# A layer norm's variance summed with tokens on the partitions, and its reciprocal spread by diagonals and a product with ones

## The chip, the cores and the metric

The kernel runs on one core of one Trainium2 chip. The metric is the device time of one execution in microseconds (us). The engines are TensorE (PE in the profile, PEld its weight loads), VectorE (DVE), ScalarE (ACT), GpSimd (POOL) and SyncE (SP, which here only issues DMAs).

## The reference

A two-layer trunk over 512 frames and 16 meta tokens, 528 tokens of 1024 channels in fp32. Layer 0 mixes with a convolution group and a pooling group, layer 1 with gated linear attention, and a squared-ReLU MLP follows each. The change lies in layer 0's mixer. Cut to what matters:

```python
a = a_in[..., :CONV_DIM] * jax.nn.sigmoid(a_in[..., CONV_DIM:])
a = causal_depthwise_conv(a, conv_w, conv_b)          # 512 channels, 31 taps
a = jax.nn.silu(layer_norm(a, ln_g, ln_b))            # mean and variance over the 512 channels of each token
...
return jnp.concatenate([a, p], axis=-1) @ w_out       # p: the pooling group's 512 channels
# layer_norm: xc * rsqrt(mean(xc * xc) + EPS) * g + b
```

## The kernel before

**Layout.** Activations lie with channels on the 128 partitions and the 528 tokens along the free dimension, so `conv` is four tiles of 128x528 (CT = 4) and a sum over channels is a sum over the four tiles and over the partitions. Each exact fp32 product is three passes over a split of both operands: weights `w_hi`, `w_lo` and activations `a_hi`, `a_lo` (`exact`, L1872), where ScalarE makes the hi part of a half block of weights (`split_hi`, L525) and VectorE the lo part (`split_lo`, L532).

**PSUM.** It is cut into NS = 4 slots of two banks. `plan_slots` numbers every accumulator of the program in the order in which TensorE fills them, and the n-th lies in slot n % 4. `start_slot(n)` makes TensorE wait until accumulator n-4 has been read: the semaphore `evac0` to `evac3` of that slot, which the engine that reads an accumulator last increments. `filled(eng, n)` is the wait in the other direction. So which read a TensorE tile waits for is set by its distance of four in that order alone.

**Order.** Each engine's program is written out by hand and runs in order. Around the change TensorE fills, in this order: `outp` 0 to 2 (the output projection of the pooling half, one 128x528 tile of 24 matmul instructions for each k), `mean`, `outp` 3 and 4, `var`, `outp` 5 to 7, then `outc` 0 to 7 (the same projection of the convolution half, which needs the normed convolution as `a_hi`, `a_lo`), then the MLP of layer 0. With the accumulator of `mean` called m, these are `outp` 3 = m+1, `outp` 4 = m+2, `var` = m+3, `outp` 5 = m+4, `outp` 6 = m+5, `outp` 7 = m+6, `outc` 0 = m+7, `outc` 1 = m+8.

**The norm.** VectorE subtracts the mean from the four tiles (L1421), ScalarE squares them (L880), VectorE adds the squares to one tile `centred_sq_sum` (L1425, L1429, a part of `h_sq`). TensorE multiplies it with `ones_c`, a 128x128 tile of 1/512 (`plain`, L1880), which leaves the variance of each token in all 128 partitions. ScalarE takes the root of that 128x528 tile into `std` (L886), VectorE the reciprocal into `rstd` (`recip`, L1252) and multiplies the four tiles with it (L1436). ScalarE applies Silu (L889), and for each of the four tiles VectorE makes `a_lo` (L1442) and, but for the first, `a_hi` (L1440). TensorE starts `outc` 0 with a wait for the first `a_lo` (`c_lo_ready`), and its four steps j wait for one `a_lo` each.

**The residual.** Each `outp` accumulator is added to `h` by VectorE (`add_to_h`, L1266), which frees its slot. `out_pool(k)` is this addition and, for odd k, one `split_lo`.

Of the kernel before, what the change touches and what calls it, by code (L numbers as in the profile page):

```python
# [17 lines left out]
ALU = mybir.AluOpType  # L18
ACT = mybir.ActivationFunctionType
# [91 lines left out]
def plan_slots():  # L111
# [5 lines left out]
    order += [("conv", 2)] + [("p", g) for g in range(PG)]  # L117
    order += [("mix", 0), ("mix", 1), ("conv", 3), ("mix", 2), ("mix", 3)]
    order += [("outp", k) for k in range(OUT_MEAN)] + [("mean",)]
    order += [("outp", k) for k in range(OUT_MEAN, OUT_VAR)] + [("var",)]  # L120
    order += [("outp", k) for k in range(OUT_VAR, KD)] + [("outc", k) for k in range(KD)]
    slot = {}

    def add(names):
# [83 lines left out]
def build_trunk(nc, x, meta_tokens, mix_norm_g, ffn_norm_g, ffn_w1, ffn_w2, cp_w_in, cp_conv_w,  # L208
                cp_conv_b, cp_ln_g, cp_ln_b, cp_pool_w, cp_pool_scale, cp_w_out, gla_w_in,
                gla_gate_w2, gla_gate_b, gla_head_g, gla_w_out, final_norm_g, out):  # L210
    with ExitStack() as ctx:
# [3 lines left out]
        def sem(name):  # L215
            return ctx.enter_context(nc.semaphore(name))
# [197 lines left out]
        o_sq_ready = sem("o_sq_ready")  # L414
        o_sq_summed = sem("o_sq_summed")
        diag_set = sem("diag_set")
        head_rows_ready = sem("head_rows_ready")
        head_normed = sem("head_normed")
        gated = sem("gated")
# [4 lines left out]
        dve_out = sem("dve_out")  # L424
        stored = sem("stored")
        N_CONST = 13
        WARM = 16

        def filled(eng, n):

            eng.wait_ge(filled_n, n + 1)

        def evacuated(eng, n):

            eng.wait_ge(evac[n % NS], n // NS + 1)
# [17 lines left out]
        def slot_ap(n, tokens=FULL, rows=P):  # L453
            a, b = pcols(tokens)
            return ps[0:rows, n % NS, a:b]
# [71 lines left out]
        def split_lo(n):  # L527

            dve = nc.vector
            half_free(dve, n)  # L530
            dve.wait_ge(w_hi_ready, group(n) + 1)
            dve.tensor_tensor(w_view(w_lo, n), half_view(raw, n), w_view(w_hi, n).bitcast(F32),  # L532
                              ALU.subtract).then_inc(w_lo_ready, 1)
# [203 lines left out]
        def _(act):  # L737
# [145 lines left out]
                    split_hi(2 * B_OUTC + k // 2)  # L883
            n = SLOT["var",]
            filled(act, n)
            act.activation(std[:, :], slot_ap(n), ACT.Sqrt, bias=eps[:, :]).then_inc(evac[n % NS], 1)  # L886
            for c in range(CT):
                act.wait_ge(normed, c + 1)
                act.activation(work[c], conv[:, c, :], ACT.Silu, bias=vec[:, V_LB + c:V_LB + c + 1],  # L889
                               scale=vec[:, V_LG + c:V_LG + c + 1]).then_inc(silu_ready, 1)  # L890
                if c == 0:

                    act.wait_ge(silu_ready, 1)
                    act.activation(a_hi[:, c, :], work[c], ACT.Copy).then_inc(c_hi_ready, 1)
# [314 lines left out]
        def _(dve):  # L1209
# [39 lines left out]
            def recip(n, tokens):  # L1249

                evacuated(dve, n)
                V.reciprocal(rstd[:, tokens[0]:tokens[1]], std[:, tokens[0]:tokens[1]])\  # L1252
                 .then_inc(rstd_ready, 1)
                uses[0] += 1
                dve.wait_ge(rstd_ready, uses[0])
# [154 lines left out]
            def out_pool(k):  # L1410
                add_to_h(k, SLOT["outp", k], FULL)
                if k % 2:
                    split_lo(2 * B_OUTC + k // 2)
# [12 lines left out]
            for c in range(2, CT):  # L1426
                dve.wait_ge(ln_sq_ready, c + 1)
                dve.wait_ge(ln_sq_summed, c - 1)
                V.tensor_tensor(centred_sq_sum, centred_sq_sum, work[c], ALU.add).then_inc(ln_sq_summed, 1)  # L1429
            split_lo(2 * B_OUTP + 3)  # L1430
            split_lo(2 * B_OUTC)
            for k in range(OUT_MEAN, OUT_VAR):
                out_pool(k)
            recip(SLOT["var",], FULL)
            for c in range(CT):
                V.tensor_tensor(conv[:, c, :], conv[:, c, :], rstd[:, :], ALU.mult).then_inc(normed, 1)  # L1436
            for c in range(CT):
                if c:
                    dve.wait_ge(silu_ready, c + 1)
                    V.tensor_copy(a_hi[:, c, :], work[c]).then_inc(c_hi_ready, 1)  # L1440
                dve.wait_ge(c_hi_ready, c + 1)
                V.tensor_tensor(a_lo[:, c, :], work[c], a_hi[:, c, :].bitcast(F32), ALU.subtract)\  # L1442
                 .then_inc(c_lo_ready, 1)
            for k in range(OUT_VAR, KD):
                out_pool(k)
            for k in range(KD):
# [398 lines left out]
        def _(pe):  # L1845
# [30 lines left out]
            def plain(n, pairs, tokens):  # L1876

                for i, (l, r) in enumerate(pairs):
                    for c, a, b in parts(tokens):
                        last = mm(ps[:, n % NS, c:c + b - a], l, r[:, a:b], start=(i == 0),  # L1880
                                  stop=(i == len(pairs) - 1))
                last.then_inc(filled_n, 1)
# [166 lines left out]
            for k in range(KD):  # L2049
                if k == OUT_MEAN:  # L2050

                    n = SLOT["mean",]
                    start_slot(n)
                    pe.wait_ge(conv_summed, 2)
                    plain(n, [(ones_c[:, :], late_sum), (ones_c[:, :], conv_sum)], FULL)
                if k == OUT_VAR:
                    n = SLOT["var",]
                    start_slot(n)
                    pe.wait_ge(ln_sq_summed, CT - 1)
                    plain(n, [(ones_c[:, :], centred_sq_sum)], FULL)  # L2060
                project_out0("outp", B_OUTP, k, PG, lambda j: evacuated(pe, SLOT["mix", j]))
            for k in range(KD):
                project_out0("outc", B_OUTC, k, 0, lambda j: pe.wait_ge(c_lo_ready, j + 1))
# [345 lines left out]
```

## Time and profile before

| | us |
|---|---|
| median of 3 runs | 1080.72 (1080.23 to 1080.99) |
| the profiled execution, its time | 1080.46 |
| its span, first to last instruction | 1078.7 |
| TensorE busy | 1067.3 (99%) |
| VectorE busy | 806.2 (75%) |
| ScalarE busy | 530.6 (49%) |

The span is that of the trace; the time holds 1.76 us more around it. The busy shares are averages over all stages; the change lies between 114 and 139 us of the span, and is read there. In a timeline row the first number is the start from the span's start, the second the duration of the group, and a bracket at the end is the idle time of that engine just before it. Records of one engine overlap by some hundredths, so the distance of two starts is what an instruction costs in a row of others.

### The profile page before, as it was taken

How to read it: one execution, taken by the hardware profiler on the slowest of the kernel's cores; microseconds unless marked ns; L12 is line 12 of the kernel's file. 1: busy time of each engine (PE TensorE's matmuls, PEld its weight loads, DVE VectorE, ACT ScalarE, POOL GpSimd, SP SyncE). 2: the span in 40 equal slices, each digit the busy share in tenths (PEclk: the TensorE clock that was granted, in tenths of full speed). 3: DMA queues.
4: the chain of work that ended last, by engine and by line, in shares of the span. 5: the costliest groups of instructions: out<-in, count | busy, mean ns of one | idle time of the engine just before them, and what ended most of it. 6: DMA issues, size and time to landing. Idle time of an engine off the chain costs nothing.

```text
span 1078.7 us, 19613 instructions
## 1 busy us (share of the span) xinstructions
PE 1067.3 (99%) x8190; PEld 992.5 (92%) x8190; DVE 806.2 (75%) x1161; ACT 530.6 (49%) x794; POOL 30.9 (3%) x85
## 2 busy tenths in 40 slices
PE   8999999999999999999999999999999999999997
PEld 8998999999999999999999877787898898898897
DVE  6899987876786786789563468757886896796785
ACT  7324454544454454467652256535544454454564
POOL 5050000000000000000000000000000000000000
PEclk9999999999999999999999999999999999999999
DMA  7361222234134125222232222222234135134121
GB/s 219 118 159 45 79 79 79 79 108 127 39 118 137 60 80 156 79 77 81 79 118 80 78 79 79 80 78 90 66 103 133 40 118 156 40 117 131 66 79 79
DMA packets 100469, 102.76 MB, mean 95 GB/s; under 512 B 3803, under 2 KB 96717, under 8 KB 100381
## 3 DMA queue, kind: packets, MB, share of 16 engines
q1 hardware_dynamic: 98780, 99.12, 29.5%
q0 software_dynamic: 1536, 2.32, 1.0%
q8 instruction: 65, 1.06, 0.4%
q14 instruction: 24, 0.19, 0.1%
q10 hardware_dynamic: 64, 0.07, 0.0%
HBM read 97.12 MB, written 2.10 MB: 92 GB/s over the span
## 4 chain that ended last, share of the span: by engine, by line
PE 95%; DVE 3%; ACT 1%; issue 0%; DMA 0%; DVEq 0%; ACTq 0%
PE ps L1872 56%; PE ps L2090 28%; PE ps L2161 4%; PE ps L2019 1%; PE ps L2122 1%; PE ps L1919 1%; PE ps L2254 1%; PE ps L2273 1%; PE ps L1880 1%; DVE w_lo L532 0%; ACT conv L775 0%; DMA xin<-in_x_dram 0%; PE ps L2149 0%; PE ps L2192 0%; DVE w_lo L571 0%
## 5 line engine op out<-in xcount | busy, mean ns | idle before, releaser
L1872 PE MATMUL ps<-u_lo,w_hi 128*128 128x264 f32 (+1 forms) x1120 | 299.5, 323 | 1.7 <-DVE u_lo L1299 1.7
L1872 PE MATMUL ps<-u_hi,w_hi 128*128 128x264 f32 (+1 forms) x1120 | 295.2, 320 | 0.0
L1872 PE MATMUL ps<-u_hi,w_lo 128*128 128x264 f32 (+1 forms) x1120 | 294.8, 319 | 0.0
L2090 PE MATMUL ps<-c_lo,w_hi 128*128 128x264 f32 (+1 forms) x868 | 245.9, 283 | 0.3 <-DVE w_lo L571 0.3
L2090 PE MATMUL ps<-c_hi,w_hi 128*128 128x264 f32 (+1 forms) x868 | 244.9, 282 | 0.0
L2090 PE MATMUL ps<-c_hi,w_lo 128*128 128x264 f32 (+1 forms) x868 | 244.7, 282 | 0.0
L525 ACT ACTIVATE w_hi<-raw 128x1024 fp32r<-128x1024 f32 x118 | 123.7, 1057 | 162.6 <-PE ps L1872 135.0
L1872 PEld LDWEIGHTS ps<-u_lo,w_hi 128*128 128x128 f32 x1120 | 184.8, 188 | 20.2 <-issue 4.8
L1872 PEld LDWEIGHTS ps<-u_hi,w_hi 128*128 128x128 f32 x1120 | 185.9, 188 | 16.5 <-issue 1.2
L1872 PEld LDWEIGHTS ps<-u_hi,w_lo 128*128 128x128 f32 x1120 | 185.5, 188 | 15.4
L532 DVE TENSOR_TENSOR w_lo<-raw,w_hi 128x1024 fp32r<-128x1024 f32 x118 | 143.7, 1223 | 64.8 <-ACT w_hi L525 63.1
L2090 PEld LDWEIGHTS ps<-c_lo,w_hi 128*128 128x128 f32 x868 | 163.4, 188 | 0.9 <-DVE w_lo L571 0.5
L2090 PEld LDWEIGHTS ps<-c_hi,w_hi 128*128 128x128 f32 x868 | 163.5, 188 | 0.2
L2090 PEld LDWEIGHTS ps<-c_hi,w_lo 128*128 128x128 f32 x868 | 163.3, 188 | 0.0
L932 ACT ACTIVATE c_hi<-parts 128x528 fp32r<-128x528 f32 (+3 forms) x132 | 73.4, 577 | 88.9 <-DVE parts L1500 51.4
L1487 DVE TENSOR_TENSOR c_lo<-parts,c_hi 128x528 fp32r<-128x528 f32 (+3 forms) x132 | 81.7, 625 | 30.2 <-ACT c_hi L932 23.7
L571 DVE TENSOR_TENSOR w_lo<-s_sum,w_hi 128x1024 fp32r<-128x1024 f32 x62 | 75.8, 1222 | 10.4 <-ACT w_hi L563 10.0
L1468 DVE SCALAR_TENSOR_TENSOR relu<-ps,rstd 128x528 f32<-128x528 f32 (+1 forms) x64 | 44.7, 698 | 47.3 <-PE ps L1872 47.2
L563 ACT ACTIVATE w_hi<-s_sum 128x1024 fp32r<-128x1024 f32 x62 | 65.7, 1059 | 13.5 <-PE ps L1872 9.9
L563 ACT ACTIVATE w_hi<-raw 128x1024 fp32r<-128x1024 f32 (+1 forms) x62 | 52.5, 846 | 37.7 <-PE ps L2090 30.4
L571 DVE TENSOR_TENSOR w_lo<-raw,w_hi 128x1024 fp32r<-128x1024 f32 (+1 forms) x62 | 59.1, 953 | 9.3 <-ACT w_hi L563 9.3
L1340 DVE SCALAR_TENSOR_TENSOR conv<-conv_in,cw,conv 128x528 f32<-128x528 f32 x66 | 47.0, 764 | 0.3
(266 smaller groups left out, 1306.5 us busy)
## 6 DMA issues: line engine op xcount, KB each, us to landing
raw<-in_ffn_w_dram SPq DMA_DIRECT2D x64, 1024.0 KB, 5.5
raw<-in_gla_w_in_dram SPq DMA_DIRECT2D x12, 1024.0 KB, 5.4
raw<-in_cp_w_in_dram SPq DMA_DIRECT2D x8, 512.0 KB, 5.4
raw<-in_cp_w_out_dram SPq DMA_DIRECT2D x4, 1024.0 KB, 5.2
raw<-in_gla_w_out_dram SPq DMA_DIRECT2D x4, 1024.0 KB, 5.1
shifted<-conv_in POOLq DMA_DIRECT2D x32, 69.5 KB, 2.1
xin<-in_x_dram SPq DMA_DIRECT2D x4, 512.0 KB, 5.5
raw<-in_cp_w_in_dram SPq DMA_DIRECT2D x2, 1024.0 KB, 5.0
```

The source lines that it names most:

```text
L525: act.activation(w_view(w_hi, n), half_view(raw, n), ACT.Copy).then_inc(w_hi_ready, 1)
L532: dve.tensor_tensor(w_view(w_lo, n), half_view(raw, n), w_view(w_hi, n).bitcast(F32), ALU.subtract).then_inc(w_lo_ready, 1)
L563: act.activation(hi, src, ACT.Copy).then_inc(w_hi_ready, 1)
L571: dve.tensor_tensor(lo, src, hi.bitcast(F32), ALU.subtract).then_inc(w_lo_ready, 1)
L932: act.activation(c_hi[:, first:last + 1, j, 0:w], now[:, first:last + 1, :], ACT.Copy)\
L1340: V.scalar_tensor_tensor(out=conv[:, c, :], in0=src, scalar=wt, in1=conv[:, c, :], op0=ALU.mult, op1=ALU.add).then_inc(tap_done[c], 1)
L1468: V.scalar_tensor_tensor(out=relu[:, i % 2, a:b], in0=slot_ap(n, tokens), scalar=0.0, in1=rstd[:, a:b], op0=ALU.max, op1=ALU.mult)\
L1487: V.tensor_tensor(c_lo[:, first:last + 1, j, 0:w], now[:, first:last + 1, :], c_hi[:, first:last + 1, j, 0:w].bitcast(F32), ALU.subtract)\
L1872: last = mm(ps[:, n % NS, c:c + b - a], l, r[:, a - origin:b - origin], start=(k == 0 and i == 0), stop=(k == count - 1 and i == 2))
L1880: last = mm(ps[:, n % NS, c:c + b - a], l, r[:, a:b], start=(i == 0), stop=(i == len(pairs) - 1))
L2090: last = mm(bank, l[:, 0, j, :], r, start=(fresh and j == 0 and m == 0), stop=(j == KD // 2 - 1 and m == 2), skip_group_check=not fresh)
L2161: last = mm(ps[:, n % NS, 0:256], l, r, start=(k == 0 and i == 0), stop=(k == KD - 1 and i == 2))
```

## The change

TensorE now multiplies with the operands in the other order: five matmuls, each with 128 tokens of `centred_sq_sum` as weights and one column of `ones_c` as the moving operand, give the variance with tokens on the partitions, 128x5 (`VAR_AT` holds the first token of each; the fifth overlaps the fourth and is there for the last 16 tokens). ScalarE's root and VectorE's reciprocal work on 128x5. VectorE then writes diagonals of the reciprocals into `std` (four 128x128 blocks in one instruction, and 16 columns in a second), and TensorE multiplies them with `ones_1` in a new accumulator `spread`, which holds the reciprocal of each token in all partitions. VectorE's four products read it from PSUM.

On VectorE the small reciprocal and the diagonals stand ahead of the additions of `outp` 3 and 4, `split_lo(2 * B_OUTC)` behind these, and `split_lo(2 * B_OUTC + 1)` behind the four `a_lo`. On TensorE `spread` stands between `outp` 5 and `outp` 6.

```diff
--- before.py
+++ after.py
@@ -117,8 +117,8 @@
     order += [("conv", 2)] + [("p", g) for g in range(PG)]
     order += [("mix", 0), ("mix", 1), ("conv", 3), ("mix", 2), ("mix", 3)]
     order += [("outp", k) for k in range(OUT_MEAN)] + [("mean",)]
-    order += [("outp", k) for k in range(OUT_MEAN, OUT_VAR)] + [("var",)]
-    order += [("outp", k) for k in range(OUT_VAR, KD)] + [("outc", k) for k in range(KD)]
+    order += [("outp", k) for k in range(OUT_MEAN, OUT_VAR)] + [("var",), ("outp", OUT_VAR), ("spread",)]
+    order += [("outp", k) for k in range(OUT_VAR + 1, KD)] + [("outc", k) for k in range(KD)]
     slot = {}
 
     def add(names):
@@ -414,6 +414,7 @@
         o_sq_ready = sem("o_sq_ready")
         o_sq_summed = sem("o_sq_summed")
         diag_set = sem("diag_set")
+        var_rows_ready = sem("var_rows_ready")
         head_rows_ready = sem("head_rows_ready")
         head_normed = sem("head_normed")
         gated = sem("gated")
@@ -424,6 +425,7 @@
         dve_out = sem("dve_out")
         stored = sem("stored")
         N_CONST = 13
+        VAR_AT = [P * t for t in range(TT)] + [TOK - P]
         WARM = 16
 
         def filled(eng, n):
@@ -883,9 +885,12 @@
                     split_hi(2 * B_OUTC + k // 2)
             n = SLOT["var",]
             filled(act, n)
-            act.activation(std[:, :], slot_ap(n), ACT.Sqrt, bias=eps[:, :]).then_inc(evac[n % NS], 1)
+            act.activation(std_tok[:, :], ps[:, n % NS, 0:TT + 1], ACT.Sqrt, bias=eps[:, :]).then_inc(evac[n % NS], 1)
             for c in range(CT):
-                act.wait_ge(normed, c + 1)
+                if c < CT - 1:
+                    act.wait_ge(normed, c + 1)
+                else:
+                    evacuated(act, SLOT["spread",])
                 act.activation(work[c], conv[:, c, :], ACT.Silu, bias=vec[:, V_LB + c:V_LB + c + 1],
                                scale=vec[:, V_LG + c:V_LG + c + 1]).then_inc(silu_ready, 1)
                 if c == 0:
@@ -1428,12 +1433,22 @@
                 dve.wait_ge(ln_sq_summed, c - 1)
                 V.tensor_tensor(centred_sq_sum, centred_sq_sum, work[c], ALU.add).then_inc(ln_sq_summed, 1)
             split_lo(2 * B_OUTP + 3)
+            evacuated(dve, SLOT["var",])
+            V.reciprocal(rstd_tok[:, :], std_tok[:, :]).then_inc(var_rows_ready, 1)
+            dve.wait_ge(var_rows_ready, 1)
+            V.tensor_tensor(std[:, 0:SEQ].rearrange("p (t n) -> p t n", n=P),
+                            ident[:, None, :].to_broadcast([P, TT, P]),
+                            rstd_tok[:, 0:TT, None].to_broadcast([P, TT, P]), ALU.mult).then_inc(var_rows_ready, 1)
+            V.tensor_scalar(std[:, SEQ:], ident[:, P - META:], rstd_tok[:, TT:TT + 1], None,
+                            ALU.mult).then_inc(var_rows_ready, 1)
+            for k in range(OUT_MEAN, OUT_VAR):
+                add_to_h(k, SLOT["outp", k], FULL)
             split_lo(2 * B_OUTC)
-            for k in range(OUT_MEAN, OUT_VAR):
-                out_pool(k)
-            recip(SLOT["var",], FULL)
+            n = SLOT["spread",]
+            filled(dve, n)
             for c in range(CT):
-                V.tensor_tensor(conv[:, c, :], conv[:, c, :], rstd[:, :], ALU.mult).then_inc(normed, 1)
+                V.tensor_tensor(conv[:, c, :], conv[:, c, :], slot_ap(n), ALU.mult)\
+                 .then_inc(normed if c < CT - 1 else evac[n % NS], 1)
             for c in range(CT):
                 if c:
                     dve.wait_ge(silu_ready, c + 1)
@@ -1441,6 +1456,7 @@
                 dve.wait_ge(c_hi_ready, c + 1)
                 V.tensor_tensor(a_lo[:, c, :], work[c], a_hi[:, c, :].bitcast(F32), ALU.subtract)\
                  .then_inc(c_lo_ready, 1)
+            split_lo(2 * B_OUTC + 1)
             for k in range(OUT_VAR, KD):
                 out_pool(k)
             for k in range(KD):
@@ -2057,7 +2073,15 @@
                     n = SLOT["var",]
                     start_slot(n)
                     pe.wait_ge(ln_sq_summed, CT - 1)
-                    plain(n, [(ones_c[:, :], centred_sq_sum)], FULL)
+                    for t, a in enumerate(VAR_AT):
+                        last = mm(ps[:, n % NS, t:t + 1], centred_sq_sum[:, a:a + P], ones_c[:, 0:1],
+                                  start=True, stop=True)
+                    last.then_inc(filled_n, 1)
+                if k == OUT_VAR + 1:
+                    n = SLOT["spread",]
+                    start_slot(n)
+                    pe.wait_ge(var_rows_ready, 3)
+                    plain(n, [(ones_1[:, :], std)], FULL)
                 project_out0("outp", B_OUTP, k, PG, lambda j: evacuated(pe, SLOT["mix", j]))
             for k in range(KD):
                 project_out0("outc", B_OUTC, k, 0, lambda j: pe.wait_ge(c_lo_ready, j + 1))
```

The new accumulator moves the numbers behind it: `outp` 5 = m+4 as before, `spread` = m+5, `outp` 6 = m+6, `outp` 7 = m+7, `outc` 0 = m+8, `outc` 1 = m+9.

TensorE at the start of `outc` 0, before (the waits of an instruction in brackets; `ps` is the accumulator):

```order
L1872 MATMUL ps<-a_hi,w_lo 128x264 x2
L1872 MATMUL ps<-a_lo,w_hi 128x264 [waits c_lo_ready,evac3,w_lo_ready]
L1872 MATMUL ps<-a_lo,w_hi 128x264
L1872 MATMUL ps<-a_hi,w_hi 128x264 x2
L1872 MATMUL ps<-a_hi,w_lo 128x264 x2
L1872 MATMUL ps<-a_lo,w_hi 128x264 [waits c_lo_ready]
```

and of the changed kernel at the same place:

```order
L1888 MATMUL ps<-a_hi,w_lo 128x264 x2
L1888 MATMUL ps<-a_lo,w_hi 128x264 [waits c_lo_ready,evac0,w_lo_ready]
L1888 MATMUL ps<-a_lo,w_hi 128x264
L1888 MATMUL ps<-a_hi,w_hi 128x264 x2
L1888 MATMUL ps<-a_hi,w_lo 128x264 x2
L1888 MATMUL ps<-a_lo,w_hi 128x264 [waits c_lo_ready]
```

The instruction that opens `outc` 0 waited for slot 3, which `var` had held; it now waits for slot 0, which `outp` 5 holds.

VectorE from the last `split_lo` ahead of the norm's second half to the addition of `outp` 5 and beyond, before (L1266 is the addition to `h`, L532 a `split_lo`):

```order
L532 TENSOR_TENSOR w_lo<-raw,w_hi 128x4x256 [waits w_hi_ready,filled] x2
L1266 TENSOR_TENSOR h<-h,ps 128x528 [waits filled]
L532 TENSOR_TENSOR w_lo<-raw,w_hi 128x4x256 [waits w_hi_ready,filled]
L1266 TENSOR_TENSOR h<-h,ps 128x528 [waits filled]
L1252 RECIPROCAL rstd<-std 128x528 [waits evac3]
L1436 TENSOR_TENSOR conv<-conv,rstd 128x528 [waits rstd_ready]
...
L1440 CAST a_hi<-act 128x528 [waits silu_ready]
L1442 TENSOR_TENSOR a_lo<-act,a_hi 128x528 [waits c_hi_ready]
L1266 TENSOR_TENSOR h<-h,ps 128x528 [waits filled]
L532 TENSOR_TENSOR w_lo<-raw,w_hi 128x4x256 [waits w_hi_ready,filled]
```

and now:

```order
L534 TENSOR_TENSOR w_lo<-raw,w_hi 128x4x256 [waits w_hi_ready,filled]
L1437 RECIPROCAL rstd_tok<-std_tok 128x5 [waits evac3]
L1439 TENSOR_TENSOR std<-ident,rstd_tok 128x512 [waits var_rows_ready]
L1442 TENSOR_SCALAR std<-ident,rstd_tok 128x16
L1271 TENSOR_TENSOR h<-h,ps 128x528 [waits filled] x2
L534 TENSOR_TENSOR w_lo<-raw,w_hi 128x4x256 [waits w_hi_ready,filled]
L1450 TENSOR_TENSOR conv<-conv,ps 128x528 [waits filled]
...
L1457 TENSOR_TENSOR a_lo<-act,a_hi 128x528 [waits c_hi_ready]
L534 TENSOR_TENSOR w_lo<-raw,w_hi 128x4x256 [waits w_hi_ready,filled]
L1271 TENSOR_TENSOR h<-h,ps 128x528 [waits filled]
L534 TENSOR_TENSOR w_lo<-raw,w_hi 128x4x256 [waits w_hi_ready,filled]
```

Behind the last `a_lo` there stood the addition of `outp` 5 and then a `split_lo`; now a `split_lo`, the addition of `outp` 5, and a `split_lo`.

## Rows read from the trace of the kernel before

**Rows 1.** The page: the span.

```profile
span 1078.7 us, 19613 instructions
```

**Rows 2.** The chain in order of time: start us, us, what.

```profile
116.05 2.55 DVE conv L1421 x4
...
126.09 3.37 DVE rstd L1252
...
136.00 28.01 PE ps L1872 x228
```

**Rows 3.** Timeline of TensorE, 121 to 137 us: start us, us, instruction.

```profile
121.69 1.05 PE L1880 MATMUL ps<-h_sq,ones_c 128*128 128x264 f32 x4
122.38 0.60 PE L1872 MATMUL ps<-a_lo,w_hi 128*128 128x264 f32 x2
...
125.49 0.40 PE L1872 MATMUL ps<-a_lo,w_hi 128*128 128x264 f32 x2
...
131.09 0.40 PE L1872 MATMUL ps<-a_hi,w_lo 128*128 128x264 f32 x2
132.82 0.48 PE L1872 MATMUL ps<-a_lo,w_hi 128*128 128x264 f32 x2 [1.33 <-DVE a_lo L1442]
133.14 0.40 PE L1872 MATMUL ps<-a_hi,w_hi 128*128 128x264 f32 x2
...
136.84 0.41 PE L1872 MATMUL ps<-a_lo,w_hi 128*128 128x264 f32 x2
```

**Rows 4.** Timeline of VectorE, 121 to 137 us.

```profile
121.37 2.35 DVE L532 TENSOR_TENSOR w_lo<-raw,w_hi 128x1024 fp32r<-128x1024 f32 x2
...
126.01 3.45 DVE L1252 RECIPROCAL rstd<-std 128x528 f32<-128x528 f32 x1
129.49 2.57 DVE L1436 TENSOR_TENSOR conv<-conv,rstd 128x528 f32<-128x528 f32 x4
131.97 0.70 DVE L1442 TENSOR_TENSOR a_lo<-relu,a_hi 128x528 fp32r<-128x528 f32 x1
...
135.24 0.71 DVE L1442 TENSOR_TENSOR a_lo<-act,a_hi 128x528 fp32r<-128x528 f32 x1
135.86 0.70 DVE L1266 TENSOR_TENSOR h<-h,ps 128x528 f32<-128x528 f32 x1
136.48 1.22 DVE L532 TENSOR_TENSOR w_lo<-raw,w_hi 128x1024 fp32r<-128x1024 f32 x1
```

**Rows 5.** Timeline of ScalarE: the root of the variance.

```profile
122.78 0.70 ACT L886 ACTIVATE std<-ps,eps 128x528 f32<-128x528 f32 x1 [1.25 <-PE ps L1880]
```

**Rows 6.** Timeline of TensorE in layer 1, a sum with tokens on partitions.

```profile
515.57 0.95 PE L1914 MATMUL ps<-ones_d,sq_sum 128*128 128x1 f32 x8
516.38 1.14 PE L1880 MATMUL ps<-sq_sum,ones_d 128*128 128x264 f32 x4
```

**Rows 7.** Timeline of ScalarE in layer 1, the root of that sum.

```profile
516.55 0.26 ACT L763 ACTIVATE std_tok<-ps,eps 128x4 f32<-128x4 f32 x1 [0.53 <-PE ps L1914]
```

**Rows 8.** Groups of VectorE in layer 1: busy us, mean ns of one.

```profile
L1709 DVE TENSOR_TENSOR act<-ident,rstd_head 128x512 f32<-128x512 f32 x2 | 1.4, 692 | 0.1
...
L1706 DVE RECIPROCAL rstd_head<-std_head 128x4 f32<-128x4 f32 x2 | 0.3, 174 | 0.0
```

**Rows 9.** Stretches: PE, PEld, DVE, ACT, POOL busy us, granted clock, DMA share, GB/s.

```profile
13.00:14.00 1.00, 0.00 (x0) 0.00 (x0) 1.00 (x3) 1.00 (x2) 1.00 (x3) 1.00 1.29 227
...
1073.00:1074.00 1.00, 0.00 (x0) 0.00 (x0) 0.94 (x3) 0.78 (x2) 0.00 (x0) 1.00 1.01 406
1074.00:1075.00 1.00, 0.00 (x0) 0.00 (x0) 0.43 (x2) 0.30 (x2) 0.00 (x0) 0.70 0.39 148
```

**Rows 10.** Timeline of SyncE's DMA issues, 118 to 150 us.

```profile
125.50 14.95 SPq L616 DMA_DIRECT2D raw<-in_ffn_w_dram  x2
```

**Rows 11.** Timeline of ScalarE: the first split of the MLP's weights.

```profile
145.87 1.06 ACT L525 ACTIVATE w_hi<-raw 128x1024 fp32r<-128x1024 f32 x1 [2.72 <-PE ps L1872]
```

**Rows 12.** DMA issues of the page: KB each, us to landing.

```profile
raw<-in_ffn_w_dram SPq DMA_DIRECT2D x64, 1024.0 KB, 5.5
```

## The prediction

> **What bounds the kernel now.** I began with the page's span [rows 1] and then read the chain of work in order of time, because the change touches one short stage and shares over the whole span say nothing of it. From 116.05 us the chain lies on VectorE, through the reciprocal at 126.09, up to the last `a_lo`, and from 136.00 on TensorE [rows 2]. So in this stage VectorE decides when TensorE gets its operands for `outc` 0. The price of that on TensorE is in its timeline [rows 3]: `outp` 6 and 7 take 2.92 us each (125.49 to the end of their 24 matmuls; the last pair starts at 131.09, and pairs follow each other at 0.24, so the tiles end at 131.33). `outc` 0 could start there. It starts at 132.82, after an idle time of 1.33, and then meets three more `a_lo` one by one; `outc` 1 starts at 136.84. A tile that waits for nothing takes 2.92, so 136.84 - 131.33 - 2.92 = 2.59 us are lost. That is all that a shorter VectorE chain could win here. From 136.00 TensorE is the chain for 28.01 us and 228 matmuls, 0.123 each, its own pace: a shift of `outc` 1 is carried on, neither given back nor made larger.
>
> **TensorE, what is removed and added.** `var` starts at 121.69 and `outp` 5 at 122.38, which gives 0.69 for the old product [rows 3]. The new one has the form of a sum in layer 1: four such matmuls start at 515.57 and the next work at 516.38, 0.81 for four, 0.20 each [rows 6]. Five take 1.01, so `outp` 5 starts at 122.70. Behind a plain product it took 125.49 - 122.38 = 3.11 [rows 3]; behind the small ones it is between 2.92 and 3.11, and I take 3.11: 125.81. There `spread` stands, the old form again, 0.69: `outp` 6 starts at 126.50, takes 3.11, `outp` 7 takes 2.92, and both are done at 132.53. TensorE has 1.20 us more to do ahead of `outc` 0 than before (1.0 with the lower values). Before, this would have lain inside the 2.59 lost.
>
> **The new chain to the four products.** The root can start 516.55 - 515.57 = 0.98 after four small matmuls began [rows 6, 7], with a fifth 1.18, at 122.87, and takes 0.26: 123.13. VectorE begins its last `split_lo` of this place at 121.37 and is free at 122.50 (two take 2.35, one lasts 1.22, so they follow at 1.13) [rows 4]. The reciprocal of a few columns takes 0.17, the diagonals have a twin in layer 1 with 0.69 [rows 8]; the 16 columns have none, and I bound them by the small reciprocal, 0 to 0.17. With hand-overs of 0.1 the diagonals stand at about 124.2. TensorE comes to `spread` at 125.81, so this wait isn't felt. Then VectorE adds `outp` 3 and 4 (0.62 each: 135.86 to 136.48 for one [rows 4]) and does a `split_lo`, 1.13: free at about 126.6. `spread` is readable 122.78 - 121.69 = 1.09 after it starts [rows 3, 5], at 126.90. So TensorE sets the start of the four products, at 126.90 against 129.49 before [rows 4], with VectorE 0.3 behind as the next bound. The removed reciprocal of 3.45 thus brings 2.59 us on VectorE. If the small steps cost up to 0.3 more, nothing changes; above that each tenth costs a tenth.
>
> **The products from PSUM.** Before they read both operands from SBUF, 2.57 for four [rows 4]; the subtraction of the mean has the new form, one operand from PSUM, and takes 2.55 [rows 2]. I take no difference.
> The Trainium skill (VectorE: DVE Perf Modes, the section on the TRN2 errata) gives a PSUM source a fixed cost 62 cycles of 0.96 GHz above an SBUF source. By that, an estimate of 0.26 us for the four would be added to the loss below; the rows of this trace show no such difference, and I go by them.
>
> **What TensorE then waits for.** The four `a_lo` move with the products: the first ends at 131.97 + 0.70 - 2.59 = 130.08, the last at 133.36. TensorE comes at 132.53 and needs the last one 3/4 of a tile later, at 134.7. So none of these is waited for any more. But the order fences show that the opening instruction of `outc` 0 now waits for slot 0, which `outp` 5 holds: the extra accumulator `spread` has put `outc` 0 at a distance of four from `outp` 5, where before it was `var`, long read. The read that frees it is VectorE's addition of `outp` 5. Before, this addition stood right behind the last `a_lo`, and only `outc` 1 waited for it (135.86 + 0.70 = 136.56, just ahead of 136.84). Now a `split_lo` has been moved ahead of it, and everything of the norm's chain stands there too. VectorE: after the last `a_lo` 135.86 - 2.59 = 133.27, `split_lo` 1.13, 134.40, addition 0.70, 135.10. With 0.05 to 0.15 for the hand-over (the first `a_lo` ended at 132.67 and TensorE started at 132.82 [rows 3, 4]) `outc` 0 starts at 135.20. TensorE is idle from 132.53 for 2.7 us, in one piece. Then the tile runs without a wait, 2.92 and 0.08 for the first pair after a wait (132.82 to 133.14 is 0.32 against 0.24): `outc` 1 starts at 138.20, where before it was 136.84.
>
> **The sum:** +1.36 us. The profiled execution took 1080.46, of which 1078.7 are span and the rest unchanged around it, so the changed kernel would take 1081.8; on the median of the runs, which is 0.26 above the profiled one, 1082.1. I give 1082.0. Both ends of the terms: `outp` 5 at 2.92 instead of 3.11 and a hand-over of 0.05 make +1.1; diagonals that are 0.5 late, or 0.1 more for each small step, make +1.7. For the case itself that is 1081.6 to 1082.6.
>
> **What hides the rest.** The MLP's first weights are loaded when VectorE has split both halves of the block that lay in that buffer: issued at 125.50 before [rows 10], now behind the moved `split_lo`, at about 134.4. A load lands 5.5 later [rows 12], at 140; ScalarE uses it at 145.87 when TensorE has finished `outc` 3 [rows 11], now at about 147. With this 7 us of cover gone it would cost one for one. `outp` 6 waits for the read of `outp` 4 (about 125.5, TensorE comes at 126.5), and `outc` 1 for that of `spread`, at about 129.5. ScalarE has less to do.
>
> **The rivals.** (1) *The stall doesn't bind and the shorter chain is gained.* `outc` 0 starts at 132.53 and `outc` 1 at 135.45, 1.39 earlier than before: 1079.3. For it speaks that VectorE's chain really becomes 2.59 shorter; against it, that the addition of `outp` 5 would have to be read by 132.53, 2.6 us before VectorE's program reaches it. This is the faster side; it decides only if the addition ends ahead of 132.5. (2) *The clock falls in the long wait.* In the rows the granted clock is 1.00 through the idle microsecond from 13 to 14 and through the first idle one behind the last matmul, 1073 to 1074, and 0.70 on average in the next, where it goes to the lower of its two levels [rows 9]. A wait of 2.7 us is longer than what these rows show without a fall. Its price: at 1.2 GHz pairs would start at twice 0.24, so a single tile of 2.92 costs 2.9 more: 1085.0.
> The Trainium skill (TensorE: Matmul & The Clock Gate, "Why this matters for your kernels") asks to avoid long idle gaps between bursts, since the clock gate then goes back to half rate; ahead of the fall at the end this trace has small matmuls and waits as well as the idle time, which here dense tiles replace, so I hold the fall unlikely. (3) *The loss is given back.* If TensorE had idle time behind `outc` 1 that waits for something not moved, it would be absorbed: 1080.7, no change. The 228 matmuls at 0.123 leave none. (4) *The diagonals or the small matmuls cost far more than their twins*, by 1 us: the products start 0.7 later, +2.1, 1082.8.
>
> **How the numbers follow.** The forecast has 0.74, rival 1 0.06, rival 2 0.06, rival 3 0.07, rival 4 0.07. A measurement of this kernel can tell about 0.2% from no change, 2.16 us; the forecast is a loss of 0.13%. Faster by more than that has 0.03 (rival 1 alone doesn't reach it), slower 0.13 (rival 2, half of rival 4, and a tail of the forecast), the rest, 0.84, is the same. The range for 8 in 10 reaches from 1080.6, so that it takes in rival 3, to 1083.3, rival 4 and what it may add; it leaves out rivals 1 and 2.
>
> **What would show it.** In the timeline of TensorE: five small matmuls in about 1.0 us; `spread` near 125.8; one idle time of 2.5 to 2.9 us ahead of the first matmul of `outc` 0, released by VectorE's L1271, an addition to `h`, and no waits inside the tile. On VectorE: products from about 126.9, and the order last `a_lo`, `split_lo`, addition. The granted clock at 1.00 from 132 to 142. The prediction is wrong if that idle time is released by an `a_lo`, if the addition comes ahead of TensorE, or if the distance between the start of `outc` 1 and the end of the span isn't that of before.

## The result, and the profile after

| | median us | range | executions |
|---|---|---|---|
| kernel before | 1080.72 | 1080.23 to 1080.99 | 7 |
| changed kernel | 1083.94 | 1082.88 to 1084.58 | 7 |

The ratio is 1.0031, with a 95% interval of 1.0021 to 1.0041: the changed kernel is 3.2 us slower. The forecast was 1.3 us slower (1082.0, from a sum of +1.36, with a range up to 1083.3): the sign was right, and the size was less than half of what was measured. The profiled execution took 1083.94, of which 1082.1 are span.

The timeline of TensorE in the changed kernel, to be held against [rows 3]. Its code lines have moved: L1888 was L1872 and L1896 was L1880.

```profile
121.76 1.17 PE L2077 MATMUL ps<-ones_c,h_sq 128*128 128x1 f32 x10
122.79 0.49 PE L1888 MATMUL ps<-a_lo,w_hi 128*128 128x264 f32 x2
...
125.79 1.05 PE L1896 MATMUL ps<-std,ones 128*128 128x264 f32 x4
126.48 0.60 PE L1888 MATMUL ps<-a_lo,w_hi 128*128 128x264 f32 x2
...
132.28 0.41 PE L1888 MATMUL ps<-a_hi,w_lo 128*128 128x264 f32 x2
135.17 0.48 PE L1888 MATMUL ps<-a_lo,w_hi 128*128 128x264 f32 x2 [2.48 <-DVE w_lo L534]
135.48 0.40 PE L1888 MATMUL ps<-a_hi,w_hi 128*128 128x264 f32 x2
...
135.96 0.44 PE L1888 MATMUL ps<-a_lo,w_hi 128*128 128x264 f32 x2
136.20 0.64 PE L1888 MATMUL ps<-a_hi,w_hi 128*128 128x264 f32 x2
136.64 0.64 PE L1888 MATMUL ps<-a_hi,w_lo 128*128 128x264 f32 x2
...
139.67 0.41 PE L1888 MATMUL ps<-a_lo,w_hi 128*128 128x264 f32 x2
```

A pair is one group of two matmuls, and a tile has twelve; the thirteenth is the first of the next tile. The reader should see two things. The last pair of `outp` 7 starts at 132.28, and `outc` 0 opens at 135.17 behind an idle time of 2.48 us. And from the fifth pair on the pairs follow at 0.44 us instead of 0.24, so that `outc` 1 starts at 139.67: the tile took 4.50 us where a free one takes 2.92.

VectorE at the same place, beside [rows 4]:

```profile
126.88 2.54 DVE L1450 TENSOR_TENSOR conv<-conv,ps 128x528 f32<-128x528 f32 x4 [0.20 <-PE ps L1896]
...
132.60 0.71 DVE L1457 TENSOR_TENSOR a_lo<-act,a_hi 128x528 fp32r<-128x528 f32 x1
133.23 1.22 DVE L534 TENSOR_TENSOR w_lo<-raw,w_hi 128x1024 fp32r<-128x1024 f32 x1
134.37 0.70 DVE L1271 TENSOR_TENSOR h<-h,ps 128x528 f32<-128x528 f32 x1
```

The four products start at 126.88, 2.61 us earlier than before, and the last `a_lo` ends at 133.31. TensorE waits on. The profile names the split at L534 as its releaser, but that one ended at 134.45; the addition behind it ends at 134.37 + 0.70 = 135.07, and TensorE starts 0.10 later. An inferred releaser that has long been done is to be read with the order of the program beside it.

Why the tile is slow is in the stretches of 1 us (the columns of [rows 9]):

```profile
135.00:136.00 1.00, 0.83 (x7) 0.86 (x8) 1.00 (x2) 0.00 (x0) 0.00 (x0) 1.00 0.35 84
136.00:137.00 1.00, 1.00 (x8) 1.00 (x7) 1.00 (x3) 0.00 (x0) 0.00 (x0) 0.59 0.81 168
137.00:138.00 1.00, 1.00 (x7) 1.00 (x6) 1.00 (x2) 0.00 (x0) 0.00 (x0) 0.50 1.03 332
138.00:139.00 1.00, 1.00 (x6) 1.00 (x6) 0.56 (x1) 0.00 (x0) 0.00 (x0) 0.50 1.07 382
139.00:140.00 1.00, 1.00 (x8) 1.00 (x7) 0.12 (x1) 0.00 (x0) 0.00 (x0) 0.70 0.59 136
```

TensorE's granted clock goes from 1.00, which is 2.4 GHz, to 0.50, 1.2 GHz, soon after 136, when it is already working again, and returns in the last of these. But in the same stretches the DMA share is high as well: the weight load that the moved split released. Both could slow the tile, which is what the second experiment separates.

Last, the end of the kernel. SyncE's waits in the last 20 us of the changed kernel (us in total, times, longest):

```profile
SPq L211 <- DMA out_dram<-y_tok: 4.0, 1, 4.0
```

and of the kernel before:

```profile
SPq L211 <- DMA out_dram<-y_tok: 3.1, 1, 3.1
```

From the start of `outc` 1 to the end of the span it is 1082.1 - 139.67 = 942.43 us now and was 1078.7 - 136.84 = 941.86: 0.57 more, with 0.9 more in the wait for the last store and a little less between. So the last of the prediction's own signs of being wrong was there: this distance was to be that of before.

### The profile page after: what moved, and what is told of

It reads as the page before. It is cut to its first block, busy times and chain, and to the rows that moved or that the text cites. A ratio compares the mean times of both kernels' runs of the same rounds, so it can differ in the third digit from the quotient of the medians.

```text
span 1082.1 us, 19636 instructions
## 1 busy us (share of the span) xinstructions
PE 1069.1 (99%) x8200; PEld 995.2 (92%) x8200; DVE 803.3 (74%) x1163; ACT 529.9 (49%) x794; POOL 30.8 (3%) x85
## 4 chain that ended last, share of the span: by engine, by line
PE 94%; DVE 2%; DMA 1%; ACT 1%; POOL 1%; issue 1%; DVEq 0%; ACTq 0%; POOLq 0%
PE ps L1888 56%; PE ps L2114 28%; PE ps L2185 4%; PE ps L2035 1%; PE ps L2146 1%; PE ps L1935 1%; PE ps L2297 1%; PE ps L2278 1%; POOL shifted L735 1%; PE ps L1896 1%; ACT conv L777 0%; DMA shifted<-conv_in 0%; DMA xin<-in_x_dram 0%; PE ps L2173 0%; PE ps L2216 0%
## 5 line engine op out<-in xcount | busy, mean ns | idle before, releaser
L1888 PE MATMUL ps<-u_lo,w_hi 128*128 128x264 f32 (+1 forms) x1120 | 299.4, 323 | 1.7 <-DVE u_lo L1304 1.7
L1888 PE MATMUL ps<-u_hi,w_hi 128*128 128x264 f32 (+1 forms) x1120 | 295.2, 320 | 0.0
L1888 PE MATMUL ps<-u_hi,w_lo 128*128 128x264 f32 (+1 forms) x1120 | 294.7, 319 | 0.0
L1888 PEld LDWEIGHTS ps<-u_lo,w_hi 128*128 128x128 f32 x1120 | 184.8, 188 | 20.2 <-issue 4.8
L1888 PEld LDWEIGHTS ps<-u_hi,w_hi 128*128 128x128 f32 x1120 | 185.9, 188 | 16.5 <-issue 1.2
L1888 PEld LDWEIGHTS ps<-u_hi,w_lo 128*128 128x128 f32 x1120 | 185.5, 188 | 15.4
L534 DVE TENSOR_TENSOR w_lo<-raw,w_hi 128x1024 fp32r<-128x1024 f32 x118 | 143.6, 1222 | 64.2 <-ACT w_hi L527 64.0
```

Of the source, the lines that this page charges most:

```text
L1888: last = mm(ps[:, n % NS, c:c + b - a], l, r[:, a - origin:b - origin], start=(k == 0 and i == 0), stop=(k == count - 1 and i == 2))
```

## The experiments

The experiments were timed against the kernel before in five rounds each, but the fourth, which had three.

| run | median us | ratio to before, 95% | `var` to `outc` 1, us | last store's wait, us |
|---|---|---|---|---|
| kernel before | | 1 | 15.15 | 3.1 |
| changed kernel | 1083.94 | 1.0031 (1.0021 to 1.0041) | 17.91 | 4.0 |
| e1_add_first | 1081.45 | 1.0011 (1.0002 to 1.0020) | 15.27 | 4.0 |
| e2_fill_the_wait | 1082.49 | 1.0021 (1.0012 to 1.0030) | 16.42 | 4.0 |
| e3_spread_in_var_slot | 1079.65 | 0.9994 (0.9985 to 1.0003) | 13.69 | 4.0 |
| e4_before_extra_slot | 1085.50 | 1.0046 (1.0031 to 1.0061) | 20.35 | 3.1 |
| e5_before_dve_pad | 1080.35 | 0.9999 (0.9990 to 1.0008) | 15.15 | 3.1 |
| e6_before_pe_pad | 1080.71 | 1.0003 (0.9995 to 1.0012) | 15.15 | 3.1 |
| e7_var_slot_dve_pad | 1079.02 | 0.9987 (0.9978 to 0.9996) | 13.69 | 3.1 |
| e8_add_ahead | 1080.18 | 0.9996 (0.9987 to 1.0005) | 13.69 | 4.0 |
| e9_before_dve_pad8 | 1080.42 | 1.0001 (0.9991 to 1.0010) | 15.14 | 3.1 |
| e10_after_dve_pad | 1083.24 | 1.0026 (1.0017 to 1.0035) | 17.94 | 3.2 |
| e11_fill_and_pad | 1082.03 | 1.0014 (1.0006 to 1.0023) | 16.40 | 3.2 |

The fourth column is read from the profiled execution of each run: from the start of the matmuls of `var` to the start of `outc` 1. The start of `var` itself moves by up to 1.2 us from one profiled execution to another (121.49 to 122.71), so single starts are to be compared with that in mind; the distance is not touched by it. It is the same to 0.03 us wherever this stage is the same.

The kernel before, run beside them, had medians of 1080.37 (e1 to e4), 1080.45 (e5 to e8) and 1080.36 (e9 to e11).

### The addition first

```diff
             split_lo(2 * B_OUTC + 1)
-            for k in range(OUT_VAR, KD):
+            split_lo(2 * B_OUTC + OUT_VAR // 2)
+            for k in range(OUT_VAR + 1, KD):
                 out_pool(k)
```

with `add_to_h(OUT_VAR, SLOT["outp", OUT_VAR], FULL)` put ahead of the first of these lines.

> The changed kernel with one swap on VectorE: behind the last a_lo the addition of outp 5 comes first, then the two weight splits. Theory (slot wait plus clock): the addition ends 1.1 us earlier, TensorE starts outc 0 at about 134.05 instead of 135.17, its idle time is about 1.4 us instead of 2.5, the granted clock stays at 1.00 through the tile, and outc 1 starts at 137.05 to 137.15: 2.5 us ahead of the changed kernel, within 0.3 us of the kernel before (1080.7 to 1081.2). Rival A (the loss beyond the stall is not the clock but something in outc 0 itself, for example contention with the weight load): the tile still takes 4.5 us, outc 1 at 138.5, 1082.4. Rival B (the additional time is made elsewhere, in the tail): only 1.1 us better than the changed kernel, 1082.8.

Timeline of TensorE:

```profile
132.16 0.40 PE L1890 MATMUL ps<-a_hi,w_lo 128*128 128x264 f32 x2
133.91 0.48 PE L1890 MATMUL ps<-a_lo,w_hi 128*128 128x264 f32 x2 [1.35 <-issue]
...
136.90 0.40 PE L1890 MATMUL ps<-a_lo,w_hi 128*128 128x264 f32 x2
```

The profile names no releaser here ("issue"). The addition starts at 133.11, ends at 133.81, and TensorE starts 0.10 later, the same 0.10 as above. The idle time is 1.35 us, the clock stays at 1.00, the tile takes 2.99, and `outc` 1 starts at 136.90, 2.8 us ahead of the changed kernel. So one instruction of 1.13 us on VectorE had cost TensorE twice: itself, and the clock. The time, 1081.45, is above the 1080.7 to 1081.2 expected, which the store's wait, 4.0 here too, would account for.

### Matmuls in the wait

```diff
+            n = SLOT["spread",]
+            evacuated(pe, n)
+            pe.wait_ge(w_lo_ready, group(2 * B_OUTC) + 1)
+            busy = half_view(w_hi, 2 * B_OUTC)[:, 0, 0:P]
+            for _ in range(10):
+                for c, a, b in parts(FULL):
+                    mm(ps[:, n % NS, c:c + b - a], busy, a_hi[:, PG, a:b], start=True, stop=True)
             for k in range(KD):
                 project_out0("outc", B_OUTC, k, 0, lambda j: pe.wait_ge(c_lo_ready, j + 1))
```

> The changed kernel with 20 matmuls of outc 0's shape and kind put in front of outc 0, into the slot of the next tile (the spread accumulator's, read by then); their results are thrown away. They take 2.43 us and fit into the idle time of 2.5 us, so the start of outc 0 stays where it is, at 135.2. Clock theory: the granted clock stays at 1.00, outc 0 takes 3.0 instead of 4.5 us, outc 1 starts at 138.2, 1.5 us better than the changed kernel: 1082.4, and 1.4 us slower than before, the forecast. Rival A (contention of outc 0 with the weight load from HBM that now falls on it): the tile takes 4.5 us as before, no gain, 1083.9, with the clock at 1.00.

```profile
132.76 2.58 PE L2092 MATMUL ps<-a_hi,w_hi 128*128 128x264 f32 x20
135.40 0.48 PE L1888 MATMUL ps<-a_lo,w_hi 128*128 128x264 f32 x2
...
138.40 0.41 PE L1888 MATMUL ps<-a_lo,w_hi 128*128 128x264 f32 x2
```

The work begins 0.2 us later in this execution, and `outc` 0 opens at 135.40, again 0.10 behind the addition. Nothing of the useful work was moved, and the tile takes 3.00 instead of 4.50. The stretches say why, and that the DMA isn't it:

```profile
137.00:138.00 1.00, 1.00 (x10) 1.00 (x10) 1.00 (x3) 0.00 (x0) 0.00 (x0) 1.00 0.92 291
138.00:139.00 1.00, 1.00 (x10) 1.00 (x9) 1.00 (x2) 0.00 (x0) 0.00 (x0) 1.00 1.07 380
```

The same weight load lies on the tile, with a share of 1.07 and 380 GB/s, at a clock of 1.00. Rival A of this run is out.

### The spread product in the variance's slot

The order is again that of the kernel before, and the product gets semaphores of its own:

```diff
-    order += [... + [("var",), ("outp", OUT_VAR), ("spread",)]
+    order += [... + [("var",)]
...
-            act.activation(std_tok[:, :], ps[:, n % NS, 0:TT + 1], ACT.Sqrt, ...).then_inc(evac[n % NS], 1)
+            act.activation(std_tok[:, :], ps[:, n % NS, 0:TT + 1], ACT.Sqrt, ...).then_inc(var_read, 1)
...
-                    n = SLOT["spread",]
-                    start_slot(n)
+                    n = SLOT["var",]
```

> The changed kernel without a new accumulator number: the product with ones is written into the slot of the variance, which has been read by then, with semaphores of its own, so outc 0 is again four behind the variance's slot, freed by the fourth product on VectorE at about 129.4. VectorE's order stays that of the changed kernel. Theory (the number of the slot makes the stall): TensorE goes from outp 7 into outc 0 at about 132.5 with no idle time, outc 1 at 135.5, 1.3 to 1.4 us ahead of the kernel before: 1079.3. Rival C (the split moved ahead of the addition, or the chain of the a_lo, holds TensorE anyway): idle time of 1 us or more ahead of outc 0 or inside it, 1080.5 or above.

```profile
132.01 0.41 PE L1890 MATMUL ps<-a_hi,w_lo 128*128 128x264 f32 x2
132.25 0.40 PE L1890 MATMUL ps<-a_lo,w_hi 128*128 128x264 f32 x2
...
135.18 0.40 PE L1890 MATMUL ps<-a_lo,w_hi 128*128 128x264 f32 x2
```

TensorE has no idle time here: the opening pair of `outc` 0 starts at 132.25 and that of `outc` 1 at 135.18, 1.66 us ahead of the kernel before. Of that, 0.20 is an earlier start of this whole stage in this execution (its five small matmuls begin at 121.49, where `var` began at 121.69), and 1.46 is won (13.69 against 15.15). VectorE's order is the changed kernel's, with the split ahead of the addition, and costs nothing now that no tile waits for this addition. Rival C is out. The time, 1079.65, is 0.0006 of the ratio below the kernel before, with an interval that reaches to no change; part of the gain goes back in the last store, whose wait is 4.0.

### The kernel before with one accumulator more

```diff
-    order += [("outp", k) for k in range(OUT_VAR, KD)] + [("outc", k) for k in range(KD)]
+    order += [("outp", OUT_VAR), ("spare",)]
+    order += [("outp", k) for k in range(OUT_VAR + 1, KD)] + [("outc", k) for k in range(KD)]
```

TensorE fills `spare` with a second product of `centred_sq_sum` and ScalarE reads one column of it; neither is used.

> The kernel before with nothing but one accumulator more in the order, behind outp 5: a plain product whose result is not used, read by a ScalarE copy of one column. The norm and VectorE's order stay as they were. Slot theory: outc 0 waits for the addition of outp 5, which ends at 136.56, and starts at 136.7 instead of 132.8; the idle time is over 4 us, the clock falls in it, and outc 1 starts at 139.7 with the clock at 1.00, at about 141 with it halved for 3 us: 1083.5 to 1085. Rival (the distance in the order doesn't matter, TensorE only has 0.9 us more work that is hidden in the old idle time): outc 0 at 132.8, 1080.7.

```profile
133.00 0.41 PE L1876 MATMUL ps<-a_hi,w_lo 128*128 128x264 f32 x2
137.67 0.78 PE L1876 MATMUL ps<-a_lo,w_hi 128*128 128x264 f32 x2 [4.26 <-DVE h L1270]
138.25 0.64 PE L1876 MATMUL ps<-a_hi,w_hi 128*128 128x264 f32 x2
...
143.06 0.41 PE L1876 MATMUL ps<-a_lo,w_hi 128*128 128x264 f32 x2
```

With nothing of the norm changed, the idle time ahead of `outc` 0 goes from 1.33 to 4.26 us, and the profile now names the addition to `h` as its releaser. The whole stage begins 1.02 us later in this execution. The time is 1085.50, 0.5 above the range that was expected. In the stretches the clock falls inside the wait:

```profile
136.00:136.20 0.20, 0.00 (x0) 0.00 (x0) 0.20 (x1) 0.20 (x1) 0.00 (x0) 0.99 0.00 0
136.20:136.40 0.20, 0.00 (x0) 0.00 (x0) 0.17 (x2) 0.20 (x1) 0.00 (x0) 0.50 0.00 0
...
138.00:139.00 1.00, 1.00 (x6) 1.00 (x6) 1.00 (x2) 0.00 (x0) 0.00 (x0) 0.50 0.00 0
```

The whole of `outc` 0 ran at 1.2 GHz, not only 3 us of it as expected, and took 143.06 - 137.67 = 5.39 us. The DMA share is 0.00 in the last of these rows, so this tile is slow with no load beside it, the reverse of the second experiment.

### The addition ahead of the four products

```diff
             split_lo(2 * B_OUTC)
+            add_to_h(OUT_VAR, SLOT["outp", OUT_VAR], FULL)
             n = SLOT["spread",]
             filled(dve, n)
```

and the loop behind the `a_lo` as in the first experiment.

> The changed kernel with its accumulator spread in the order, and the addition of outp 5 placed ahead of the four products on VectorE. Slot theory: the slot is read at about 127.3, so outc 0 starts at 132.6 with no idle time though it stands four behind outp 5; the products start 0.3 us later than in the changed kernel, and the last a_lo is ready at 133.7, ahead of its use at 134.8: 1079.7, like the kernel with spread in the variance's slot, clock at 1.00. Rival (the number of accumulators as such, not the place of the read): idle time stays.

```profile
132.31 0.41 PE L1890 MATMUL ps<-a_hi,w_lo 128*128 128x264 f32 x2
132.55 0.40 PE L1890 MATMUL ps<-a_lo,w_hi 128*128 128x264 f32 x2
...
135.47 0.40 PE L1890 MATMUL ps<-a_lo,w_hi 128*128 128x264 f32 x2
```

The accumulator `spread` keeps its number and `outc` 0 its distance of four from `outp` 5, yet there is no idle time: `outc` 0 starts at 132.55 and `outc` 1 at 135.47, where the forecast's first rival had put it, though the products start 0.36 us later, at 127.24. So it is the place of the read that counts, not the number of accumulators. The time, 1080.18, was expected at 1079.7; the wait for the last store is 4.0 here as well.

### What the last store waits for

In the last 4 us of each of the five kernels with a wait of 4.0 there is a packet of an instruction queue among those of the store, and in none of the other eight. Queues in the last 4 us of e3:

```profile
q1 hardware_dynamic: 245, 0.87, 55.7%
q14 instruction: 1, 0.01, 0.5%
```

and of e7, which differs from it by these two lines at the start of VectorE's program, where it waits anyway:

```diff
+            for i in range(40):
+                V.memset(std[:, i:i + 1], 0.0)
```

```profile
q1 hardware_dynamic: 288, 1.05, 65.6%
```

> The kernel with spread in the variance's slot, and forty 128x1 memsets more at the start of VectorE's program, where it waits. Code theory, VectorE: the load moves forty instructions forward, out of the last store; the last wait is 3.1 and the kernel takes 0.9 us less than with no memsets, 1078.8, 1.6 below the kernel before. Rival (TensorE's code, or the number doesn't matter): 1079.7, the wait 4.0.

The packet is gone from the end, the wait is 3.1, and the ratio to the kernel before is 0.9987 instead of 0.9994. The expected time was 1078.8. From the start of `outc` 1 to the end of the span the five kernels with the packet take 942.30 to 942.93 us (mean 942.5), the eight without it 941.55 to 942.35 (mean 941.9). That the packet is what delays the store is the likeliest reading, since the two come and go together in 13 kernels; nothing moved the packet alone.

The other direction didn't succeed:

```diff
+            for i in range(3):
+                V.memset(std[:, i:i + 1], 0.0)
```

> The kernel before with three 128x1 memsets more at the start of VectorE's program, where it waits anyway (the changed kernel has two VectorE instructions more). What is asked is the tail: in all kernels with the change's code so far SyncE waits 4.0 us for the last store instead of 3.1, and a packet of the instruction queue lies among the store's packets. Code theory: an instruction load falls into the last store because VectorE's code has grown past a limit; then these three move it too, the last wait becomes 4.0, and the kernel takes 0.9 us more than before, 1081.3. Rival: it is TensorE's code, or not the code at all; then 1080.4, no difference, and a wait of 3.1.

```diff
-        WARM = 16
+        WARM = 21
```

> The kernel before with five warm-up products more at the start of TensorE's program (ten instructions, the number that the change adds there), 1.0 us of which 0.3 are idle time and the rest is covered by later waits for VectorE in the first 15 us. If TensorE's code makes the instruction load fall into the last store, the last wait is 4.0 and the kernel takes 0.9 us more, 1081.3; if VectorE's does, 3.1 and 1080.4 to 1080.7.

> The kernel before with eight 128x1 memsets at the start of VectorE's program instead of three. The code theory for VectorE is half open: forty of them took the instruction load out of the last store, three did not bring it in. If the limit lies between three and eight, the last wait becomes 4.0 and the kernel takes 0.9 us more, 1081.3. If it stays at 3.1 and 1080.4, this says only that the limit isn't there.

In all three (the last with `range(8)`) the wait stays at 3.1 and the time is that of the kernel before. So forty instructions more on VectorE take the packet out of the store (here, in e10 and in e11), and what brought it in with the change was not found: neither three nor eight instructions more on VectorE do it, nor ten on TensorE.

### The changed kernel without the tail, and without both

The changed kernel with the forty memsets:

> The changed kernel with forty 128x1 memsets at the start of VectorE's program. Code theory: the last wait falls from 4.0 to 3.1 and the kernel takes 0.9 us less, 1083.0; the stall and the fall of the clock at outc 0 stay, with outc 1 at 139.7. Rival: the tail is tied to the change otherwise, 1083.9.

The wait is 3.2, the time 1083.24, 0.0005 of the ratio below the changed kernel's, and the stall is there, 2.48 us. The clock falls earlier in this execution and returns earlier, so that already the second pair is slow and the last three are not:

```profile
135.36 0.63 PE L1890 MATMUL ps<-a_lo,w_hi 128*128 128x264 f32 x2 [2.48 <-DVE w_lo L534]
135.79 0.64 PE L1890 MATMUL ps<-a_hi,w_hi 128*128 128x264 f32 x2
...
139.89 0.40 PE L1890 MATMUL ps<-a_lo,w_hi 128*128 128x264 f32 x2
```

`outc` 1 starts at 139.89, and the tile took 4.53 us, as in the changed kernel (4.50).

Its eleven executions reach from 1081.33 to 1084.37, wider than those of any other kernel here. The two lowest, 1081.33 and 1081.92, lie where e11's do (1081.42 to 1082.55), which has no fall. The mean granted clock of the whole execution is on record for each: 0.998 for these two and 0.996 or 0.997 for the other nine, where e11 has 0.998 or 0.999 in all of its. In the changed kernel it is 0.998 in the fastest of the seven (1082.88) and 0.996 or 0.997 in the others. So the same kernel seems to run sometimes with the fall and sometimes without; there is no trace of one without it.

With the twenty matmuls in the wait as well:

> The changed kernel with both: twenty matmuls in the wait ahead of outc 0, and the forty memsets. What is left of the change is then the stall for the slot alone, the forecast's sum: +1.36 us against before, 1081.7 to 1081.9. If a further cost is hidden it is more.

It takes 1082.03, a ratio of 1.0014, 1.5 us with an interval from 0.6 to 2.5. That is 0.1 above the 1081.7 to 1081.9 expected. This is the changed kernel with the stall for the slot alone, and what the forecast's sum had been made for: +1.36. In its trace the distance from `var` to `outc` 1 is 16.40, 1.25 more than before, and the tile takes 3.00.

## Why the prediction was wrong in its size

**Right: the slot.** That `outc` 0 would no longer wait for an `a_lo` but for the addition of `outp` 5 was shown by two kernels that undo it in different ways (e3, e8), by one that shortens it (e1), and by one that makes it with nothing else changed (e4).

**Right: the terms of the sum up to the opening of `outc` 0.** Forecast and trace: `outp` 5 at 122.70 and 122.79, `spread` at 125.81 and 125.79, the four products at 126.90 and 126.88, the addition at 134.40 and 134.37, `outc` 0 at 135.20 and 135.17. Two small misses cancelled there: `outp` 5 started 0.09 late, and took 3.00 instead of 3.11. The diagonals of 128x512 took 0.69, as their twin in layer 1. Products from PSUM took 2.54 for four, where from SBUF it had been 2.57 [rows 4]: the 0.26 us more, estimated from the Trainium skill (VectorE: DVE Perf Modes, the section on the TRN2 errata), aren't there.

**Wrong: "Then the tile runs without a wait, 2.92 and 0.08 for the first pair".** Without a wait it did run, but at half the clock for most of its length: 4.50 instead of 3.00. This was rival 2, held at 0.06. It was weighed too lightly. The evidence against it was two shorter idle times, and behind the second the clock did fall:

```profile
14.61 0.48 PE L1872 MATMUL ps<-u_lo,w_hi 128*128 128x264 f32 x2 [1.70 <-DVE u_lo L1299]
...
1072.57 0.41 PE L1919 MATMUL ps<-ident,relu 128*128 128x128 f32 x2
```

The first lasted 1.70 us, with the clock at 1.00 throughout. The second begins behind the last matmul, which ends at 1072.98. The clock of 0.70 from 1074 to 1075 [rows 9] is 1.00 for 0.4 us and 0.50 for the rest, so it fell at about 1074.4, after 1.4 us. The wait that was forecast was longer than both.

Rival 2 was also priced at a whole tile, 2.9, where the fall covered a part of it. The price is 1.5 us in both traces that can be set beside one without the fall (17.91 less 16.42 for e2, 17.94 less 16.40 for e11), 1.1 from the ratios of the changed kernel and e2 (0.0010), and 1.2 from the medians of e10 and e11. That the times give less than the traces fits with executions in which the clock didn't fall. The Trainium skill (TensorE: Matmul & The Clock Gate, "Why this matters for your kernels") asks for no long idle gaps between bursts, since the clock gate then goes back to half rate. The traces bear the rule out: an idle time of 2.48 us was followed by the fall in both executions profiled, one of 1.35 us (e1) wasn't; my reason for setting it aside, what had run ahead of the fall at the end of the old trace, was no evidence.

**Wrong: "of which 1078.7 are span and the rest unchanged around it".** The end of the kernel was taken to be rigid. The wait for the last store is 0.9 us longer, and 0.5 to 0.75 of that shows in the times (0.0005 of the ratio between the changed kernel and e10, 0.0007 between e2 and e11 and between e3 and e7). No row of before hinted at it, and what brings the packet there stays open.

**The sum again.** From the traces, `outc` 1 starts 139.67 - 136.84 = 2.83 us later: 0.07 because the whole stage began later, 1.27 for the stall (16.42 in e2 less 15.15), where the forecast had 1.36, and 1.49 for the clock (17.91 less 16.42), where it had nothing. The end adds 0.57, which makes the 3.4 us between the spans. The times divide less sharply: 1.5 for the stall (e11), 1.2 for the clock (e10 less e11) and 0.5 for the tail (the changed kernel less e10). These add up to the 3.2 us measured because each is the difference to the next, so the sum proves nothing, and each is uncertain by about 1 us, as the intervals show.

**The other rivals.** (1) didn't occur, but was right in its size: where the stall is taken away, `outc` 1 starts at 135.47 (e8), forecast 135.45. (3) didn't occur: behind `outc` 1 nothing gave the loss back. (4) didn't either: the diagonals and the small matmuls cost what their twins did.

## What to carry to other kernels

A new accumulator in a rotation over few slots changes who waits for whom for every tile behind it. List for each what stands four ahead, and where its reader's read stands in that engine's program, before costing the operation itself: here the shorter chain was worth 1.46 us at `outc` 1, and the displaced read took 4.22, stall and clock together (17.91 less 13.69). Put such a product into a slot that is already read (e3), or the read ahead of the long chain (e8). Both win the 1.46 us in the trace, but neither can be told from the kernel before by its time, since both have the packet in the last store. With it out of the way, e7 takes 1079.02, 0.9987 of the kernel before (0.9978 to 0.9996).

And a wait of TensorE costs more than its length once it is long enough for the clock to fall: here 1.35 and 1.70 us cost only themselves, 2.48 us cost 1.1 to 1.5 us on top. No run lies between 1.70 and 2.48, the kernel with 2.48 us doesn't seem to pay in every execution, and behind the last matmul, where TensorE had been busy only in part, 1.4 us were enough. So the length of the idle time alone doesn't decide.

## What the hardware showed beyond that

The clock need not fall in the wait itself. In the changed kernel it fell a microsecond after dense work had begun again (136.2), in e10 0.2 us after (about 135.5), in e4 inside the wait (136.2, 2.8 us after the last matmul had ended). So a slow tile with no idle time right in front of it can belong to a gap further back.

One packet of an instruction queue goes with a longer store: where it lies among the last store's packets, SyncE's wait is 4.0 us instead of 3.1 or 3.2, and forty memsets of 128x1 at the start of VectorE's program take both away. So a difference of some tenths of a microsecond between two builds can come from the length of their code. Here it was 0.0007 of the ratio (e3 to e7), as much as e3 had gained over the kernel before (0.0006).
